# Memory heads, decay levels and idle matmuls behind the second mixer's input product

## What is computed

```python
def hgrn2_mixer(h, mem, w_in, lb, out_norm_g, mem_norm_g, w_mem_kv, w_out):
    proj = h @ w_in
    q, fz, i, g, qm = jnp.split(proj, ...)
    f = lb + (1.0 - lb) * jax.nn.sigmoid(fz32)
    k = (1.0 - lb) * jax.nn.sigmoid(-fz32)
    # o_t = q_t S_t,  S_t = diag(f_t) S_{t-1} + k_t^T v_t, 6 heads of 128
    o = hgrn2_chunkwise(heads(q), heads(k), heads(i), heads(log_f))
    o = rms_norm(o, out_norm_g) * jax.nn.silu(heads(g).astype(F32))
    om = memory_attention(qm, mem, mem_norm_g, w_mem_kv)   # 4 heads of 64, softmax over 256
    return jnp.concatenate([o, om], axis=-1) @ w_out
```

## Time and profile before

| | |
|---|---|
| median of 3 runs | 1992.08 us (1990.87 to 2000.05) |
| profiled execution | 1990.98 us |
| span in its trace | 1989.2 us |
| TensorE busy, mean granted clock | 1850.5 us (93%), 0.945 |
| DVE, ACT, POOL busy | 1432.0, 1107.9, 109.7 us |

### The profile page before, as it was taken

One profiled execution on the slowest core, in us unless ns is written; L12 is line 12 of the kernel. 1 busy time (PEld: TensorE's weight loads), 2 busy tenths in 40 slices (PEclk: granted clock), 3 DMA queues, 4 the chain that ended last, 5 costly groups with the idle time before them and its releaser, 6 DMA issues.

```text
span 1989.2 us, 22586 instructions
## 1 busy us (share of the span) xinstructions
PE 1850.5 (93%) x8585; PEld 1521.3 (76%) x8591; DVE 1432.0 (72%) x1186; ACT 1107.9 (56%) x992; POOL 109.7 (6%) x143
## 2 busy tenths in 40 slices
PE   6979999999898999999999999999999398799995
PEld 5767788688777888888888888888888287668884
DVE  4555678667547888888888888888888543465654
ACT  5463344343316777777777777777777342433332
POOL 1010111002000000000000000000000101100000
PEclk9988999999789999999999999999999697699998
DMA  8544899653138999999999999999999652226540
GB/s 315 171 138 140 291 332 322 214 170 108 57 103 324 379 376 387 377 381 385 379 381 379 385 381 383 372 376 378 373 381 359 223 177 79 64 89 208 190 149 21
DMA packets 238733, 532.03 MB, mean 267 GB/s; under 512 B 17578, under 2 KB 41274, under 8 KB 238112
## 3 DMA queue, kind: packets, MB, share of 16 engines
q1 hardware_dynamic: 223856, 476.24, 66.5%
q0 software_dynamic: 14768, 54.36, 7.9%
HBM read 520.01 MB, written 10.53 MB: 267 GB/s over the span
## 4 chain that ended last, share of the span: by engine, by line
PE 64%; DVE 3%; ACT 1%; DMA 1%; issue 1%; POOL 0%; DVEq 0%; ACTq 0%; POOLq 0%
PE bank L2256 20%; PE bank L2257 20%; PE bank L2264 20%; PE bank L2648 1%; PE bank L2422 1%; PE bank L2283 1%; DMA kv<-rel_rows 0%; PE bank L2797 0%; PE bank L2384 0%; PE bank L2683 0%; DMA taken_b<-y_dram,y_row 0%; DVE x L2141 0%; DMA y_dram<-y_rows 0%; DVE proj L1564 0%; PE bank L2443 0%
## 5 line engine op out<-in xcount | busy, mean ns | idle before, releaser
L1408 DVE TENSOR_TENSOR w_lo<-raw,w_hi 128x2048 fp32r<-128x2048 f32 x454 | 1041.2, 2296 | 251.6 <-ACT w_hi L939 245.8
L939 ACT ACTIVATE w_hi<-raw 128x2048 fp32r<-128x2048 f32 x454 | 867.4, 1912 | 526.5 <-PE bank L2257 406.0
L2256 PE MATMUL bank<-w_hi,slot_hi 128*128 128x512 f32 x896 | 356.1, 397 | 5.1 <-ACT w_hi L939 2.6
L2257 PE MATMUL bank<-w_hi,slot_lo 128*128 128x512 f32 x896 | 350.2, 391 | 0.0
L2256 PE MATMUL bank<-w_hi,hT_hi 128*128 128x512 f32 (+2 forms) x736 | 292.5, 399 | 6.0 <-ACT w_hi L939 4.0
L2257 PE MATMUL bank<-w_hi,hT_lo 128*128 128x512 f32 (+2 forms) x736 | 288.3, 393 | 0.0
L2264 PE MATMUL bank<-w_lo,slot_hi 128*128 128x512 f32 x896 | 240.2, 390 | 0.7 <-DVE w_lo L1408 0.7
L2256 PEld LDWEIGHTS bank<-w_hi,slot_hi 128*128 128x128 f32 x896 | 168.8, 188 | 39.5 <-issue 5.9
L2264 PEld LDWEIGHTS bank<-w_lo,slot_hi 128*128 128x128 f32 x896 | 168.4, 188 | 36.6 <-DVE w_lo L1408 1.1
L2257 PEld LDWEIGHTS bank<-w_hi,slot_lo 128*128 128x128 f32 x896 | 169.0, 189 | 33.4
L2264 PE MATMUL bank<-w_lo,hT_hi 128*128 128x512 f32 (+2 forms) x736 | 180.1, 387 | 0.0
(11 more groups left out here) (319 smaller groups left out, 1535.7 us busy)
## 6 DMA issues: line engine op xcount, KB each, us to landing
raw<-in_moe_w_gate_up SPq DMA_DIRECT2D x448, 512.0 KB, 5.6
raw<-in_moe_w_down SPq DMA_DIRECT2D x224, 512.0 KB, 5.6
raw<-in_w_ff SPq DMA_DIRECT2D x64, 512.0 KB, 4.4
work<-in_w_ada POOLq DMA_DIRECT2D x48, 512.0 KB, 5.4
raw<-in_dense_w_gate_up SPq DMA_DIRECT2D x44, 512.0 KB, 5.1
raw<-in_b_w_in SPq DMA_DIRECT2D x24, 512.0 KB, 4.8
raw<-in_w_in SPq DMA_DIRECT2D x24, 512.0 KB, 5.5
raw<-in_dense_w_down SPq DMA_DIRECT2D x22, 512.0 KB, 4.9
```

The costliest lines, as they stand in the source:

```text
L939: act.activation(w_hi[:, g % SPLIT, 0:n], raw[:, g % RING, 0:n], ACT.Copy).then_inc(R.hi, 1)
L1408: dve.tensor_tensor(w_lo[:, g % SPLIT, 0:n], raw[:, g % RING, 0:n], f32(w_hi[:, g % SPLIT, 0:n]), ALU.subtract).then_inc(R.lo, 1)
L2256: pe.matmul(out_, hi, w_hi[:, s, c:c + w], start=(start and n == 0), stop=False, skip_group_check=True)
L2257: mm = pe.matmul(out_, lo, w_hi[:, s, c:c + w], start=False, stop=False, skip_group_check=True)
```

## The change

Three things. On ACT both items' exponentials run one after the other, then both `turned_out`, and `begin("b_out")` comes last. On PE `value_products(b_items[0])` goes ahead of level 6 and `value_products(b_items[1])` behind level 8 (they stood together between levels 6 and 7), and the two `turn_probs` are parted; a new function `tree_idle` puts five idle matmuls ahead of each of levels 5 to 8, behind a wait for the `keep` that frees the level's banks; 14 more stand ahead of the transposes of `mix_b`, in bank 1. On DVE `value_out(b_items[0])` goes from the end of the tree to a place between `keep(5)` and `queries(7)`.

```diff
@@ scalar
-                exponentials(b_items[0], None)
-                begin("b_out")
-                exponentials(b_items[1], None)
+                for it in b_items:
+                    exponentials(it, None)
                 for it in b_items:
                     turned_out(it, None)
+                begin("b_out")
                 load_sqrt()
@@ vector
                 keep(hgrn, 5)
+                value_out(b_items[0])
                 queries(hgrn, 7)
                 decays(hgrn, 7)
                 keep(hgrn, 6)
                 queries(hgrn, 8)
                 keep(hgrn, 7)
-                for it in b_items:
-                    value_out(it)
+                value_out(b_items[1])
@@ tensor
+            def tree_idle(d, level, count):
+
+                pe.wait_ge(*at(d.tag, "kept", level - 2))
+                run_idle(count, (4, 6)[level % 2])
@@ tensor
                 for it in b_items:
                     scores(it, None)
+                tree_idle(hgrn, 5, 5)
                 tree_level(hgrn, 5)
-                for it in b_items:
-                    turn_probs(it, None)
+                turn_probs(b_items[0], None)
+                tree_idle(hgrn, 6, 5)
+                turn_probs(b_items[1], None)
+                value_products(b_items[0], None)
                 tree_level(hgrn, 6)
-                for it in b_items:
-                    value_products(it, None)
+                tree_idle(hgrn, 7, 5)
                 tree_level(hgrn, 7)
+                tree_idle(hgrn, 8, 5)
                 tree_level(hgrn, 8)
+                value_products(b_items[1], None)
                 tree_products(hgrn)
             if have("b_out"):
                 S.stage("b_out")
-                turn_split("mix_b", mix, at("hgrn", "normed", 0),
+                turn_split("mix_b", mix, at("hgrn", "normed", 0), 14, 1,
                            later={1: at("hgrn", "normed", 1), 2: at("hgrn", "normed", 2), 3: at("mix_b")})
```

## The result

| | median us | lowest to highest, runs |
|---|---|---|
| before | 1992.05 | 1987.3 to 2000.05, 7 |
| changed | 1982.68 | 1976.36 to 1984.69, 7 |

The ratio is 0.9946, with a 95% interval of 0.993 to 0.9962: 7.6 to 13.9 us faster, 9.4 by the medians, against 11.9 forecast. Three executions in all, two of before and one of a variant, took 3750 us and more; no time, ratio or trace here counts them. The profiled execution of the changed kernel took 1980.68 us (span 1978.9) where before's took 1990.98 (1989.2): 10.3 less.

What follows compares the result with a forecast made beforehand. TensorE bounds the kernel nearly throughout, at half clock after an idle stretch. Tree 10.1 plus `b_out` 1.8 makes 11.9 us off 1990.98: 1979.1, or 1980.2 as a median, which stands 1.1 above; range 1977 to 1990.

Steps and rivals of the forecast that it cites:

- Where the kernel stood: Tree, 500 to about 521: TensorE alone sets the time, at half clock after 2.93 us idle, paying nearly double.
- The tree, 10.1 us: Scores to the tree's products: clock stays up, products start at 512.3 in place of 522.42, 10.1 us sooner.
- the four idle blocks: Five idle matmuls ahead of each of levels 5 to 8; the two last were priced as 2.2 us true cost.
- DVE and ACT hidden: In the tree, DVE's chain hides beneath PE by 0 to 1.9 us; ACT's moved weight copies cost nothing.
- `b_out`, 1.8 us: Start of `b_out`: last transposes and first 16 matmuls at the high clock, 1.5 to 2.1 us won, 1.8 taken.
- Rival 1: Clock holds through the tree, falls again ahead of `b_out`: 10.1 us alone, 1980.9, median 1982.0; chance 0.15.
- the transposes from 530.16: Ahead of `b_out`: read as not lifting the clock, so by the skill's rule the 1.8 us would not come.
- Rival 2: Clock falls in value products 0 or level 6, about 503: 1987.6, median 1988.7, or 1985 if lifted again; chance 0.17.
- the weak place: Value products 0 and level 6: 40 narrow matmuls, 4.5 us, without a wide one, where the clock might fall.
- Rival 3: Tree's idle matmuls paid at low clock, transposes 5.5 us late: slower, median 1995.8 to 1997.6; chance 0.08.
- the dip of 1728: Late in the kernel: clock 0.82 over 1728 to 1730, one of the later dips worth a microsecond or two.
- the 8 of slice 12: Page's clock line: dip read as part of the stretch that the change touches.

Runs made afterwards that it cites:

- the second set of runs: The changed kernel, unaltered, measured again in the same rounds as its variants: 1980.31 us, ratio 0.9949.
- the kernel padded by 8: The kernel before with 44 in place of 36 idle matmuls ahead of the transposes of `norm_moe`: 1995.97 us against 1993.82, ratio 1.0022.

## Why the forecast was right, and what it got wrong

- **Where the kernel stood** (TensorE at half clock from 500 behind a hole of 2.93 us): shown, by closing the hole in two other ways; that the fall would last to the end of level 8 was so in both traces of before, but is not fixed by the program (24.05 in one trace of the same code).
- **The tree, 10.1 us**: measured 10.4, for the reason given. Levels 6 and 7 came at 2.67 and 2.63 us (forecast 2.73); item 1's exponentials moved ahead of the weight copies. Inside the term the four idle blocks were priced too high: 1.4 us by the kernels without them, forecast 2.2.
- **DVE and ACT hidden**: right, with more room than worked out: queries 7 ended 2.2 us before level 7 (forecast 0.8 at the worst), ACT had 4.46 us left. No wait took the place of the one removed.
- **`b_out`, 1.8 us**: 2.2 in the two traces of the changed kernel, against the 17.53 us of before. It hangs on the clock's staying up behind the 14 idle matmuls, and in three traces with the same code there, but without the tree's 20, it fell in the last transposes, with nothing gained over the order alone (16.5 to 16.7 beside 16.68). Rival 1, given 0.15, came in those three. The two terms were also not separate, as the sum had them: the tree's 20 cost 1.4 us in one and may have been needed for the other, and with no idle matmul at all the first `w_lo` came at the same time (37.06 and 37.08).
- **A reading that was wrong**: the prediction says that the transposes from 530.16 did not lift the clock. The first four took 0.66 us, as at 1.00 in the changed kernel; the clock fell in the next four, in before's timeline of PE:

```profile
531.21 1.11 PE L2283 MATMUL bank<-con,mix 128*128 128x128 f32 x4 [0.39 <-DVE mix L1647]
```

  Behind the idle 3.45 us, then, they began high and fell to 0.50. Of the Trainium skill's rule that transposes do not count as PE being busy (TensorE: Matmul & The Clock Gate, Part 4) these traces bear out a part: behind the 14, all sixteen transposes from 517.51 ran at 1.00 in the changed kernel, against what the prediction drew from the rule. In the kernel without the tree's 20 the clock was down to 0.50 during the last eight, as the rule has it. With ACT's order alone it rose to 1.00 during sixteen others, against the rule itself.
- **Rival 2**, 0.17: refuted by 64 narrow matmuls in a row at 1.00. I had called that run the weak place; the profile of before never tested it, since its narrow work there ran low for another reason.
- **Rival 3**, 0.08: one part of its mechanism was seen in the kernel with the 14 alone, 2.2 us lost by products at the low clock and 2.2 won behind them.
- **The step that was off**: "a microsecond or two from the dips later on, whose place need not stay". In the profiled pair it was 4.6 us, the whole difference between the 12.6 won locally and the 8.1 that arrived: 2.8 ahead of the experts, the rest behind their first matmul. I named the dip of 1728 and overlooked those of `route`, although they stood in the earlier trace rows: a slice is 49.7 us long, so both dips of the tree and of `b_out` (500 to 538) lie in slice 11, and the 8 of slice 12, which I put down to the stretch of the change, is `route`'s. There before was short in both of its traces (33.1 and 33.2 us, 35.4 to 38.7 in all others). I take that for luck, since one kernel's two traces differ by 1.6 us there, but no run shows it. So 1980.2 was too low by 2.5 (1982.68; 1980.31 in the second set of runs), well inside the range.
- Faster by over 0.5%, given 0.61: by the ratio it is 0.54%, and since its interval (0.38 to 0.70%) holds 0.5%, the runs do not decide between faster and the same by that bound.

**Left open.** Why the dips fall where they do in a given execution, and why the hole was followed by 20 us and more of low clock in three traces and by a few in one. Why before's tail was the shortest twice. Whether the clock holds through the transposes of `mix_b` because of the tree's 20 idle matmuls. Why the 1.7 us saved ahead of `norm_moe` did not show in the total. And whether the kernel without the tree's idle matmuls is truly better than the changed one: in the same rounds the medians say 2.7 us (1977.57 and 1980.31), but the intervals overlap.

## What to carry to other kernels

When a stretch of PE runs at half clock, look for the idle stretch ahead of it and what ended that, and close it by moving the work that is late (here a few lines of ACT's order, which by themselves brought `w_lo` 11.4 of the 12.6 us forward) before adding idle matmuls. Here the order alone, with no idle matmul, had the first `w_lo` as early as the whole change; those in narrow but gapless work cost 1.4 us and held nothing there that needed holding. And test the parts together as well as apart: the 14 were worth 2.3 us behind the tree's 20 and nothing without them, in so few traces that it may be a draw. A local gain read from one pair of traces is not yet the kernel's gain: compare starts from a common anchor, stage by stage, and allow for the later dips by the spread of stages whose code is the same (here 33 to 39 us for one stretch). And profile each kernel twice where the argument rests on the length of a dip.

## What the runs showed of the hardware that was not expected

- Narrow matmuls (64 columns) at 0.114 us each ran at a granted clock of 1.00 throughout, here 5.52 us of 48 behind 2.00 of 16 (the order without its idle matmuls). At 0.50 they can go on low, as before from 510 to 520, or the clock can rise in their midst, as in level 6 of the kernel padded by 8.
- The clock can fall while PE is at work, some time behind a gap. In the changed kernel it fell within the router's 8-column matmuls, with no gap since 555.98, where one of 1.46 us ended (and one of 1.03 us at 553.26):

```profile
558.20 0.38 PE L2632 MATMUL bank<-w_router,hT_hi 128*128 128x8 f32 x2
558.43 0.57 PE L2632 MATMUL bank<-w_router,hT_lo 128*128 128x8 f32 x2
558.86 0.57 PE L2632 MATMUL bank<-w_router,hT_hi 128*128 128x8 f32 x2
```

  From 0.22 us to 0.43 from start to start, from one pair of matmuls to the next.
- The same instructions behind the same gap (2.92 and 2.93 us) met a low clock of 20 us and more in three executions and of a few in another; behind the same 14 idle matmuls and 1.09 us gap the clock stayed at 1.00 in both traces of the changed kernel and fell in all three without the tree's 20.
